# Root and inverse of six layer norms on two columns instead of 256

## The reference, cut to what matters

```python
def layer_norm(x, g, b):
    mu = jnp.mean(x, axis=-1, keepdims=True)
    var = jnp.mean(jnp.square(x - mu), axis=-1, keepdims=True)
    return (x - mu) * lax.rsqrt(var + LN_EPS) * g + b

def second_block(...):
    for i in range(DEPTH):                    # DEPTH = 2
        ...
        y_conv = conformer_conv(...)          # has silu(layer_norm(y, g_ln, b_ln)) over 512 channels
        mix = jnp.concatenate([y_pool, y_conv], axis=-1) @ w_out[i]
        x = layer_norm(DEEPNORM_ALPHA * x + mix, ln1_g[i], ln1_b[i])      # 1024 channels
        f = swiglu_2(...) if i % 2 == 0 else moe_swiglu(...)
        x = layer_norm(DEEPNORM_ALPHA * x + f, ln2_g[i], ln2_b[i])        # 1024 channels
        x = x + jax.nn.sigmoid(x @ ple_gate_w[i]) * (p[i] @ ple_w[i])
```

## Time and profile before

| | us |
|---|---|
| median of three runs | 2732.53 |
| lowest and highest | 2723.38, 2736.0 |
| the profiled execution, its own time | 2735.35 |
| its span, first to last instruction | 2733.9 |
| TensorE busy in the span | 2628.6 (96%) |
| VectorE busy | 2069.9 (76%) |
| ScalarE busy | 1614.8 (59%) |
| GpSimd busy | 224.5 (8%) |
| mean granted TensorE clock | 0.987 of full speed |

### The profile page before, as it was taken

The page is one execution under the profiler, slowest core; times in us unless marked ns, Lnnn a source line. Parts: engine busy times, 40 slices in busy tenths (PEclk is TensorE's granted clock), DMA queues, the critical chain, the costliest instruction groups (busy, mean ns, idle before and its releaser), DMA issues.

```text
span 2733.9 us, 43598 instructions
## 1 busy us (share of the span) xinstructions
PE 2628.6 (96%) x17668; PEld 2289.1 (84%) x17668; DVE 2069.9 (76%) x2973; ACT 1614.8 (59%) x2394; POOL 224.5 (8%) x229
## 2 busy tenths in 40 slices
PE   8999899999899999999999898999999999999997
PEld 7989889899787779998899886888888888888886
DVE  6667776776744557668655686999999999999995
ACT  5556455555332235543555535878787878778785
POOL 1101000000011127010600010000000000000000
PEclk9999999999999999999999999999999999999999
DMA  7553245555322125543355333999999999899992
GB/s 272 185 185 110 104 168 186 175 184 185 113 94 71 63 102 185 185 166 124 135 186 186 138 138 122 379 351 345 355 375 351 347 353 366 334 362 364 353 375 80
DMA packets 84605, 604.91 MB, mean 221 GB/s; under 512 B 9400, under 2 KB 9528, under 8 KB 12016
## 3 DMA queue, kind: packets, MB, share of 16 engines
q1 hardware_dynamic: 82016, 594.05, 59.3%
q10 hardware_dynamic: 2032, 4.85, 0.5%
q0 software_dynamic: 352, 3.15, 0.3%
HBM read 600.96 MB, written 1.05 MB: 220 GB/s over the span
## 4 chain that ended last, share of the span: by engine, by line
PE 87%; DVE 9%; ACT 2%; issue 1%; DMA 1%; ACTq 0%; DVEq 0%
PE bank L428 86%; DVE arena L2266 2%; DVE weights_lo L418 2%; PE bank L2856 1%; DVE arena L1200 1%; ACT weights_hi L410 1%; DVE rstd L479 1%; DMA x_T<-in_x 0%; DVE x_T L734 0%; DVE arena L2289 0%; DVE arena L555 0%; DVE arena L1202 0%; ACT x_T L546 0%; DVE arena L2980 0%; PE bank L1869 0%
## 5 line engine op out<-in xcount | busy, mean ns | idle before, releaser
L418 DVE TENSOR_TENSOR weights_lo<-raw_weights,weights_hi 128x1024 fp32r<-128x1024 f32 x816 | 1004.3, 1249 | 388.9 <-ACT weights_hi L410 383.3
L410 ACT CAST weights_hi<-raw_weights 128x1024 fp32r<-128x1024 f32 x816 | 849.4, 1050 | 333.2 <-PE bank L428 318.6
L428 PE MATMUL bank<-source,weights_hi 128*128 128x512 f32 (+1 forms) x3040 | 876.3, 356 | 43.4 <-DVE weights_lo L418 18.5
L428 PE MATMUL bank<-source,weights_lo 128*128 128x256 f32 x2400 | 682.0, 284 | 0.0
L428 PEld LDWEIGHTS bank<-source,weights_hi 128*128 128x128 f32 x3040 | 541.5, 194 | 130.9 <-issue 28.0
L428 PEld LDWEIGHTS bank<-source,weights_lo 128*128 128x128 f32 x2400 | 462.9, 193 | 0.1
L418 DVE TENSOR_TENSOR weights_lo<-arena,weights_hi 128x1024 fp32r<-128x1024 f32 x278 | 336.5, 1225 | 32.0 <-ACT weights_hi L410 28.5
L410 ACT CAST weights_hi<-arena 128x1024 fp32r<-128x1024 f32 x278 | 292.2, 1053 | 56.8 <-PE bank L428 40.3
L428 PE MATMUL bank<-weights_hi,source 128*128 128x512 f32 (+1 forms) x1024 | 309.6, 386 | 3.5 <-issue 3.0
L428 PE MATMUL bank<-hidden_hi,weights_hi 128*128 128x256 f32 x912 | 258.3, 283 | 0.0
L428 PE MATMUL bank<-hidden_lo,weights_hi 128*128 128x256 f32 x912 | 258.0, 283 | 0.0
(11 more groups left out here) (317 smaller groups left out, 3374.6 us busy)
## 6 DMA issues: line engine op xcount, KB each, us to landing
raw_weights<-in_exp_in SPq DMA_DIRECT2D x134, 1024.0 KB, 5.1
arena<-in_exp_in SPq DMA_DIRECT2D x90, 1024.0 KB, 5.0
raw_weights<-in_exp_w SPq DMA_DIRECT2D x67, 1024.0 KB, 5.1
arena<-in_exp_w SPq DMA_DIRECT2D x45, 1024.0 KB, 5.1
raw_weights<-in_ffn_w_down SPq DMA_DIRECT2D x44, 1024.0 KB, 4.9
raw_weights<-in_ffn_w_up SPq DMA_DIRECT2D x43, 1024.0 KB, 4.9
raw_weights<-in_ffn_w_gate SPq DMA_DIRECT2D x42, 1024.0 KB, 4.9
raw_weights<-in_dense_w SPq DMA_DIRECT2D x33, 1024.0 KB, 4.9
```

The costliest lines, as they stand in the source:

```text
L410: k.act.copy(k.weights(j)[0], raw_half(k, j)).then_inc(k.w_hi_ready, 1)
L418: k.dve.tensor_tensor(lo, raw_half(k, j), hi.bitcast(F32), ALU.subtract).then_inc(k.w_ready, 1)
L428: return k.pe.matmul(dst, lhsT, rhs, start=start, stop=stop, skip_group_check=shared)
```

## The change

For the six norms the squares are summed the other way round: the block of squares is the stationary operand and one column of ones the moving one, so that the sums of 128 tokens come out in one column with the tokens on the partitions; two such columns hold all 256 tokens. ScalarE takes the root of these two columns, VectorE the reciprocal of two columns and a copy that repeats each of them 128 times, and TensorE brings them back with two matmuls against the identity, so that again every partition holds each token's value. VectorE multiplies by it where it lies, in the accumulation bank. The other norms keep the old way.

```diff
--- before.py
+++ after.py
@@ -47,6 +47,7 @@
 HALVES = 4
 HALF = UNIT // 2
 LEVELS = (2, 4, 8, 16, 32)
+ROOT_BANK, CONV_ROOT_BANK = 7, 4
 N_RW_MASK = 10
 
 
@@ -487,6 +488,44 @@
                                    ALU.mult).then_inc(*k.normed.step((f, i)))
 
 
+def token_squares_tensor(k, f, bank, n_k):
+
+    for i in range(n_k):
+        k.pe.wait_ge(*k.norm_roots.at((f, "square", i)))
+        for s in range(TT):
+            ins = mm(k, k.bank[bank][:, s:s + 1], blk(k.sq, i)[:, s * P:(s + 1) * P], k.con("ones")[:, 0:1],
+                     i == 0 and s == 0, i == n_k - 1, True)
+    ins.then_inc(*k.norm_sums.step((f, "square")))
+
+
+def token_root_scalar(k, f, bank, n, eps):
+    k.act.wait_ge(*k.norm_sums.at((f, "square")))
+    k.act.activation(k.std[:, 0:TT], k.bank[bank][:, 0:TT], ACT.Sqrt, bias=k.con(eps),
+                     scale=1.0 / n).then_inc(*k.norm_roots.step((f, "std")))
+
+
+def token_root_vector(k, f):
+    inverse = k.std[:, TT:2 * TT]
+    k.dve.wait_ge(*k.norm_roots.at((f, "std")))
+    k.dve.reciprocal(inverse, k.std[:, 0:TT]).then_inc(*k.normed.step((f, "inverse")))
+    k.dve.wait_ge(*k.normed.at((f, "inverse")))
+    k.dve.tensor_copy(k.rstd[:, :].rearrange("p (s c) -> p s c", s=TT),
+                      inverse.rearrange("p (s o) -> p s o", o=1).to_broadcast([P, TT, P])).then_inc(*k.normed.step((f, "spread")))
+
+
+def spread_root_tensor(k, f, bank):
+
+    k.pe.wait_ge(*k.normed.at((f, "spread")))
+    for s in range(TT):
+        ins = mm(k, k.bank[bank][:, s * P:(s + 1) * P], k.rstd[:, s * P:(s + 1) * P], k.con("ident"), True, True)
+    ins.then_inc(*k.norm_sums.step((f, "rstd")))
+
+
+def spread_root(k, f, bank):
+    k.dve.wait_ge(*k.norm_sums.at((f, "rstd")))
+    return k.bank[bank][:, 0:T]
+
+
 def centre_tensor(k, f, z, bank, n_k, ready):
     for i in range(n_k):
         ready(i)
@@ -508,17 +547,18 @@
 def layer_norm_scalar(k, f, z, bank, n_k):
     centre_scalar(k, f, bank, n_k)
     squares_scalar(k, f, z, n_k, lambda i: k.act.wait_ge(*k.normed.at((f, "centred", i))))
-    root_scalar(k, f, bank + 1, n_k * P, "eps_ln")
+    token_root_scalar(k, f, bank + 1, n_k * P, "eps_ln")
 
 
 def layer_norm_tensor(k, f, z, bank, n_k, ready):
     centre_tensor(k, f, z, bank, n_k, ready)
-    squares_tensor(k, f, bank + 1, n_k)
+    token_squares_tensor(k, f, bank + 1, n_k)
+    spread_root_tensor(k, f, ROOT_BANK)
 
 
 def layer_norm_vector(k, f, z, n_k):
     centre_vector(k, f, z, n_k)
-    root_vector(k, f)
+    token_root_vector(k, f)
 
 
 def norm_to_x_scalar(k, f, z, gain, bias, layer):
@@ -531,8 +571,9 @@
 
 def norm_to_x_vector(k, f, z, gain, layer):
     layer_norm_vector(k, f, z, KT)
+    rstd = spread_root(k, f, ROOT_BANK)
     for i in range(KT):
-        k.dve.scalar_tensor_tensor(blk(z, i), blk(z, i), k.col(gain, layer * KT + i), k.rstd[:, :], ALU.mult,
+        k.dve.scalar_tensor_tensor(blk(z, i), blk(z, i), k.col(gain, layer * KT + i), rstd, ALU.mult,
                                    ALU.mult).then_inc(*k.normed.step((f, "scaled", i)))
 
 
@@ -2168,9 +2210,10 @@
     mixer_out_tensor(k, layer, 0, 0, ("pool", layer))
     centre_tensor(k, f, t.y, 4, 4, lambda g: k.pe.wait_ge(*k.mix_dve.at((layer, "y", g))))
     mixer_out_tensor(k, layer, 0, 1, ("pool", layer))
-    squares_tensor(k, f, 5, 4)
-    for s in range(2):
-        mixer_out_tensor(k, layer, 1, s, ("pool", layer))
+    token_squares_tensor(k, f, 5, 4)
+    mixer_out_tensor(k, layer, 1, 0, ("pool", layer))
+    spread_root_tensor(k, f, CONV_ROOT_BANK)
+    mixer_out_tensor(k, layer, 1, 1, ("pool", layer))
     for half in range(2):
         j = k.half["conv_pw_2", layer, half]
         k.pe.wait_ge(k.w_ready, j + 1)
@@ -2229,7 +2272,7 @@
     centre_scalar(k, f, 4, 4)
     squares_scalar(k, f, t.y, 4, lambda i: k.act.wait_ge(*k.normed.at((f, "centred", i))))
     split_hi(k, "w_out_2", 4 * layer, 1)
-    root_scalar(k, f, 5, 4 * P, "eps_ln")
+    token_root_scalar(k, f, 5, 4 * P, "eps_ln")
     split_hi(k, "w_out_2", 4 * layer + 1, 0)
     for g in range(4):
         k.act.wait_ge(*k.mix_dve.at((layer, "scaled", g)))
@@ -2306,9 +2349,10 @@
     k.dve.wait_ge(*k.mix_dve.at((layer, "y", 3)))
     centre_vector(k, f, t.y, 4)
     split_lo(k, "w_out_2", 4 * layer, 1)
-    root_vector(k, f)
+    token_root_vector(k, f)
+    rstd = spread_root(k, f, CONV_ROOT_BANK)
     for g in range(4):
-        k.dve.scalar_tensor_tensor(blk(t.y, g), blk(t.y, g), k.col("conv_ln_g_2", layer * 4 + g), k.rstd[:, :], ALU.mult,
+        k.dve.scalar_tensor_tensor(blk(t.y, g), blk(t.y, g), k.col("conv_ln_g_2", layer * 4 + g), rstd, ALU.mult,
                                    ALU.mult).then_inc(*k.mix_dve.step((layer, "scaled", g)))
     split_lo(k, "w_out_2", 4 * layer + 1, 0)
     for g in range(4):
```

## The result

In 20 runs each the changed kernel takes 2739.33 us (2733.36 to 2746.21) and the kernel before 2733.26: **6.1 us longer**, a ratio of 1.0024 [1.0016, 1.0032]. That is less than half a per cent, and the time is inside the range, but the forecast was 2.1 us less, so the sign was wrong. The profiled execution has a span of 2737.9 us and a mean granted clock of 0.982 (before 2733.9 and 0.987).

A forecast was written before the change was run, and what follows sets the result against it. TensorE, with 87% of the chain, was taken as the bound. Terms of -1.5 (ln1), -0.6 (ln2), -1.5 (layer 0's clock) and +1.5 (convolution) sum to -2.1 us, giving 2730.4 us; range 2720 to 2740, 8 in 10.

The forecast's parts named there:

- Root, reciprocal, spread: From root to first scaled block: 1.54 us against 2.30, so 0.76 us less a norm where on the path.
- Squares: no change: Sums of squares: 32 one-column records take 3.8 us against 3.73 for the old 16, taken as 0.
- -1.5 - 0.6 - 1.5: The four wide norms: ln1 of both layers -1.5 us, ln2 of both layers -0.6, layer 0's clock at ln2 -1.5.
- ln2: At ln2 TensorE becomes the later one and its 2.06 us of idle time goes: 0.30 us less a layer, -0.6.
- layer 0's clock: Behind ln2 of layer 0, without the idle gap, 144 records take 17.55 us instead of 19.04: -1.5 us, ends 0 and -1.5.
- The convolution: Convolution's norm, both layers: four more TensorE records (0.54 us) and a 0.2 us wait, +1.5 us, ends +0.8 and +2.4.
- the 0.2 us that the block had to spare: Convolution's norm: the first source block was done at 1284.59 and due at 1284.80, so 0.2 us early.
- Scaling from the bank: VectorE's scaling with the root read from the accumulation bank: 468 ns against 480 from memory, taken as 0.
- B: Sums of squares: weight loads set a slower pace, up to 0.23 us a record, 2749 us; chance 0.15 of above before.
- a pace of 0.16: Sums of squares: 0.16 us a record, half way to the 1.2 GHz pace, giving +4.9 us, 2737.4.
- A: At ln1 the spread matmuls cut the gap and keep TensorE at 2.4 GHz: 5.1 us more gained, 2725.3; chance 0.2.
- C: Whole change moves waits and shortens nothing: ln1 -1.5, convolution +1.5, ln2 gains nothing, sum 0, 2732.5 us; chance 0.2.

The follow-up runs named there:

- experiment 3: Changed kernel with the sums taken over 128 columns of ones instead of one, in all six norms: 2728.28 us, ratio 0.9978 to the kernel before.
- experiment 1: Changed kernel with the two convolution norms put back as before, only the four 1024-channel norms changed: 2738.61 us, ratio 1.0008 to the kernel before.
- experiment 5: The changed kernel itself, unedited, timed and profiled a second time: 2738.32 us, ratio 1.0014 to the kernel before.
- 6: Changed kernel with 128 columns of ones in the four 1024-channel norms and the convolution norms as before: 2726.61 us, ratio 0.997 to the kernel before.
- experiments 2: Changed kernel with the four 1024-channel norms put back as before, only the two convolution norms changed: 2741.41 us, ratio 1.0021 to the kernel before.
- 8: Only the two convolution norms changed, their sums over 128 columns of ones: 2739.1 us, ratio 1.0015 to the kernel before.
- 9: The kernel before with twelve tiny products added ahead of TensorE's first matmul (24 records more): 2736.86 us, ratio 1.0012 to the kernel before.
- 10: Only the two convolution norms changed (one column), with 28 tiny products ahead of TensorE's first matmul: 2737.12 us, ratio 1.0015 to the kernel before.
- 7: Changed kernel with 128 columns of ones everywhere and the convolution's spread matmuls moved into the middle of half 0: 2728.11 us, ratio 0.9977 to the kernel before.

## Why the prediction was wrong

**Root, reciprocal, spread: right in every price.** Root 0.26 (0.25 forecast), reciprocal 0.17, copy 0.29. With the clock up, as in experiment 3, root to scaled is 1.60 us for the forecast 1.54. In the changed kernel it is 2.11, because the four records cost 1.24 us at 1.2 GHz; the gain on the path is then 0.19 us and not 0.76.

**Squares: no change. This is the step that failed.** The pace was right: at the full clock 32 thin records take 3.73 to 3.75 us, for 3.8 forecast (ln2 of layer 1 in the changed kernel, two norms in experiment 1). What failed is that the clock was taken to hold. I priced the sums by their duration alone and took a TensorE that is busy without a break to be one whose clock holds. But the row I priced them from, two columns behind a load, was chosen for its length and says nothing on what many such records do to the clock. Here it falls to 0.50 while they run, and the squares take 4.7 us on the mean of the 16 thin norms (3.73 to 6.40). At ln1 of layer 0 that costs little on balance (no more than the +0.4 us, most of it from one profile), since the clock had been lost in the gap behind them anyway. At ln2, where nothing had been lost yet, it costs most: squares of 6.16 us, root and spread at 1.2 GHz, the head of the product too. In all, the four wide norms give +4.0 us by stages where the forecast had -1.5 - 0.6 - 1.5 = -3.6.

**ln2: right only where the clock holds.** The order of events is as forecast: TensorE becomes the later one and the idle time of 2.06 us goes. I expected -0.6 for both layers and -1.5 for layer 0's clock, so -1.8 and -0.3. With dense sums the stage is 2.1 us shorter in layer 0 and 1.2 in layer 1; with thin ones it is 1.6 and 1.3 us longer. In layer 1 the gain is above the forecast because three of the five profiles with the old norms lose the clock there too (39.0 to 40.1 us, against 38.4 in the two that do not, and 37.8 dense). At ln2 the forecast was for the dense kernel without saying so.

**The convolution: right mechanism, too small.** +1.5 forecast, +2.1 measured. The four records are not to blame: TensorE's next record starts 0.36 us behind their first, for 0.54 forecast, and the 0.60 us of their row includes the last one's way through. VectorE's source block sets the length: it comes 1.04 us later in the stage in experiment 5 than in 6, near the 0.98 forecast, and the product starts 1.04 us later. The term that was mis-sized is the 0.2 us that the block had to spare. The product starts 0.56 us behind the start of that block before (1284.24 and 1284.80) and in experiment 5 alike, so there was next to nothing to spare. Root and reciprocal saved here brought nothing, as said.

**Scaling from the bank: right,** 475 ns against 480. By the Trainium skill (VectorE: DVE Perf Modes, the section on the TRN2 errata) it would have been 65 ns longer, an estimate from its cycle counts; the trace does not agree.

**The rivals.** B comes nearest: "a pace of 0.16 ... +4.9, 2737.4", for which I gave 0.15. The time is right, by a mechanism that is half B's. B named the fall to 1.2 GHz "during such thin work", but saw it as the way to a pace of 0.23; with the clock mostly down it is 0.20 (6.40 / 32, experiment 1), and 4.7 / 32 = 0.15 on the mean. And B left out what the low clock does to the work behind the sums. What I held for B, squares of ln2 of layer 1 at the lower clock already before, was no evidence for it: TensorE had been idle for 3.85 us ahead of them in that profile, and in the four others with the old norms (experiments 2, 8, 9 and 10), where it was idle for 1.4 to 2.7 us, they take 3.7 us at the full clock. A falls: it took the four records for filler that could hold the clock, and in the changed kernel the clock is gone before they come. With dense sums a part of A comes true. Behind ln1 of layer 0 the clock is at 0.50 for 6.8 us in all five profiles with the old norms and in experiment 3, but for 3.4 in experiments 6 and 7, and in 6 it stays at 1.00 through the gap of layer 1, which lies in this window of its trace:

```profile
1652.00:1654.00 2.00, 0.71 (x4) 0.52 (x4) 1.20 (x4) 0.42 (x2) 0.00 (x0) 1.00 0.00 0
```

This goes with the dense stages from ln1 on, which are 1.3 and 1.8 us shorter and not only the 0.7 that the norm itself saves. The Trainium skill (TensorE: Matmul & The Clock Gate, the section on why this matters for your kernels) says that idle gaps between bursts let the clock fall and that matmuls back to back keep it; in these runs it also fell in thin matmuls back to back, which the trace shows as busy throughout. C falls, since ln1 did not bring its -1.5 and the convolution cost more than +1.5.

**The numbers.** 2739.3 lies just inside the upper end of the range, and within half a per cent of before. The range reached there through the scatter of a median, not through the case that happened, so that it held the time is luck.

## What to carry to other kernels

A sum by tokens on TensorE should be made dense: with 128 columns of ones instead of one a record costs next to nothing more (0.120 against 0.117 us at the full clock), the clock holds, and this kernel is 10 to 12 us faster (6 less than before, against 4 to 6 more). Price thin matmuls by what the clock does to the work behind them as well as by their own length, and place a small dependent matmul where its result is needed next, since one behind a long run of others passes its delay on. Compare changes of a few us by stages, and look at branches first: a program that is 24 records longer resumed about 3 us later behind one.

## What the runs showed of the hardware that was not expected

TensorE can be busy without a break by the profile and still lose its clock: 1.00 at the start of 32 records of one column, 0.50 at their end (in the records or right behind them in 16 norms of 16), and 1.00 throughout with 128 columns in the same records (12 of 12). What amount of work it takes between one column and 128 was not tried. Nor is it shown that thin work alone is enough: there is idle time of 1.4 us or more ahead of all these squares, and where 16 such records stood among dense ones, in the convolution, the clock held.

Behind the branch to the experts TensorE resumed after 3.1 to 3.7 us in nine profiles and after 6.1 to 6.8 us in three, and the three are those with exactly 24 records more than before (twice in the convolution's kernels, once in the otherwise untouched one). Longer programs, by 80 and 104 records, are back at 3.1 to 3.7 us. That the length of TensorE's program decides it is shown, with one profile of each kernel: adding 24 records to the kernel before brought the delay and adding 56 to the convolution's kernel took it away. By what means (where the target's code then lies, and how it is fetched) stays open.
